# The residual of the first token half added by DMA in two down-projections

## The reference

```
x = x + m[2] * rmsnorm(mixer(h), g_post_mix)
h = modulate(rmsnorm(x, g_pre_ffn), m[3], m[4])
x = x + m[5] * rmsnorm(conv_ffn(h, w_up, w_dw, b_dw, w_down), g_post_ffn)

def conv_ffn(h, w_up, w_dw, b_dw, w_down):
    u = depthwise_conv(h @ w_up, w_dw) + b_dw
    gate, val = split(u, 2)
    return (silu(gate) * val) @ w_down       # 2816 -> 1024
```

## Time and profile before

| | |
|---|---|
| Median of 3 runs | 2520.65 us (2512.99 to 2523.09) |
| Profiled execution | 2511.87 us, span 2510.0 us |
| Mean granted PE clock | 0.990 |
| PE busy | 2420.9 us (96%), 11028 matmuls |
| DVE busy | 1955.5 us (78%) |
| ACT busy | 1259.4 us (50%) |
| POOL busy | 1036.8 us (41%) |
| DMA | 366.32 MB, mean 146 GB/s |

### The profile page before, as it was taken

One profiled execution on the slowest core, in us unless ns is written; L12 is line 12 of the kernel. 1 busy time (PEld: TensorE's weight loads), 2 busy tenths in 40 slices (PEclk: granted clock), 3 DMA queues, 4 the chain that ended last, 5 costly groups with the idle time before them and its releaser, 6 DMA issues.

```text
span 2510.0 us, 32042 instructions
## 1 busy us (share of the span) xinstructions
PE 2420.9 (96%) x11028; PEld 1937.1 (77%) x11028; DVE 1955.5 (78%) x2537; ACT 1259.4 (50%) x2062; POOL 1036.8 (41%) x731
## 2 busy tenths in 40 slices
PE   7989999999899999999999899999999999999997
PEld 3868888888687787888788687756877878887886
DVE  4467676667648999999655879997679999996556
ACT  3356665666544555555554442244645555555542
POOL 0057677882043566666200321000435666662002
PEclk9999999999999999999999999999999999999999
DMA  6046465651531354456975577611213544559755
GB/s 267 27 143 176 136 174 155 178 151 51 180 118 51 112 142 132 126 126 135 266 238 170 172 200 188 149 34 68 101 51 108 144 135 126 126 132 268 232 173 176
DMA packets 153204, 366.32 MB, mean 146 GB/s; under 512 B 14432, under 2 KB 15712, under 8 KB 153056
## 3 DMA queue, kind: packets, MB, share of 16 engines
q1 hardware_dynamic: 107056, 242.69, 27.5%
q0 software_dynamic: 44416, 116.93, 21.7%
q10 hardware_dynamic: 1584, 4.85, 0.6%
HBM read 303.07 MB, written 136.31 MB: 175 GB/s over the span
## 4 chain that ended last, share of the span: by engine, by line
PE 45%; DVE 38%; issue 7%; POOL 4%; ACT 3%; DMA 3%; SPq 0%; ACTq 0%; DVEq 0%; POOLq 0%
DVE weights_f32r L1998 13%; PE psum L2277 13%; PE psum L2279 12%; PE psum L2278 12%; DVE low L1975 3%; DVE acts L2187 3%; DVE acts L2189 3%; DVE low L1967 3%; DVE low L1965 2%; PE psum L2493 2%; ACT weights_f32r L976 1%; POOL set L837 1%; DMA set<-mod_w 1%; DVE weights_f32r L1862 1%; PE psum L2482 1%
## 5 line engine op out<-in xcount | busy, mean ns | idle before, releaser
L2277 PE MATMUL psum<-acts_f32r,weights_f32r 128*128 128x512 f32 x1536 | 610.0, 397 | 20.6 <-DVE low L2031 6.6
L2279 PE MATMUL psum<-acts_f32r,weights_f32r 128*128 128x512 f32 x1536 | 600.0, 391 | 0.0
L2278 PE MATMUL psum<-acts_f32r,weights_f32r 128*128 128x512 f32 x1536 | 599.7, 390 | 0.0
L976 ACT ACTIVATE weights_f32r<-low 128x512 fp32r<-128x512 f32 (+2 forms) x471 | 307.3, 659 | 336.0 <-PE psum L2279 159.2
L1998 DVE TENSOR_TENSOR weights_f32r<-low,weights_f32r 128x512 fp32r<-128x512 f32 x264 | 405.2, 1579 | 1.3
L862 POOL TENSOR_TENSOR low<-low 128x512 f32<-128x512 f32 x91 | 134.7, 1481 | 654.0 <-ACT low L1215 647.6
L2277 PEld LDWEIGHTS psum<-acts_f32r,weights_f32r 128*128 128x128 f32 x1536 | 289.4, 188 | 87.5 <-DVE weights_f32r L2004 7.7
L2279 PEld LDWEIGHTS psum<-acts_f32r,weights_f32r 128*128 128x128 f32 x1536 | 289.3, 188 | 61.5
L2278 PEld LDWEIGHTS psum<-acts_f32r,weights_f32r 128*128 128x128 f32 x1536 | 289.6, 189 | 60.6 <-issue 2.4
L889 POOL TENSOR_TENSOR low<-low 128x512 f32<-128x512 f32 x150 | 258.3, 1723 | 39.8 <-DVE acts_f32r L1983 29.3
L2277 PE MATMUL psum<-high_f32r,weights_f32r 128*128 128x512 f32 (+1 forms) x485 | 195.2, 403 | 16.2 <-ACT low L976 12.7
(11 more groups left out here) (254 smaller groups left out, 4944.4 us busy)
## 6 DMA issues: line engine op xcount, KB each, us to landing
low<-units SPq DMA_DIRECT2D x130, 512.0 KB, 4.9
set<-mod_w POOLq DMA_DIRECT2D x80, 512.0 KB, 3.9
low<-gated_sums SPq DMA_DIRECT2D x110, 256.0 KB, 4.5
low<-weight_sums SPq DMA_DIRECT2D x88, 256.0 KB, 4.2
gated_sums<-low SPq DMA_DIRECT2D x22, 768.0 KB, 3.5
low<-units SPq DMA_DIRECT2D x66, 256.0 KB, 5.0
weight_sums<-units POOLq DMA_DIRECT2D x14, 1024.0 KB, 10.3
residual<-low SPq DMA_DIRECT2D x48, 256.0 KB, 2.0
```

The lines of the kernel that those rows point to most:

```text
L976: return act.activation(out, in_, ACT.Copy, scale=scale)
L2277: pe.matmul(out, wl, xh, start=first, stop=False, skip_group_check=continued)
L2278: pe.matmul(out, wh, xl, start=False, stop=False, skip_group_check=continued)
L2279: return pe.matmul(out, wh, xh, start=False, stop=last, skip_group_check=continued)
```

## The change

In `down(b)` POOL now issues, for each block k of half 0, a DMA that adds the block of `xs_d` onto `A_half(k, 0)`, after three waits: the stores of the stream have landed, the block is renewed (`y_scaled`), and DMA k - 2 has landed. For b = 1 blocks 0 to 2 stand at the first x square of half 0 and block k + 2 ahead of POOL's addition of square k; for b = 3 all eight stand ahead of the additions of half 1. The semaphores `mod_in` become `pool_in` and count on. DVE's `add_residual(b, 0, k)` for b = 1 and 3 and SP's `load_residual(b, 0)` for them go. ACT's `x_square` and SP's `store_x` wait, by `residual_added`, for the DMA's landing where they waited for DVE. `X_BEFORE` gives the counts of DVE's remaining additions.

```
--- before.py
+++ after.py
@@ -263,6 +263,7 @@
 
 
 Y_BEFORE = (0, 16, 20, 36)
+X_BEFORE = {(0, 0): 0, (0, 1): 8, (1, 1): 16, (2, 0): 24, (2, 1): 32, (3, 1): 40}
 SQ_INDEX, SQ_FREED, SQ_SUMS, STAT_BEFORE = squares()
 T_BASE = {key: CB * n for n, key in enumerate([(0, 0), (0, 1), (1, 0), (1, 1), ("ln", 0), ("ln", 1), (2, 0), (2, 1)])}
 
@@ -335,7 +336,7 @@
         silu_c = sem("silu_c")
         scale_in = [sem(f"scale_in{j}") for j in range(CB // 2)]
         shift_in = [sem(f"shift_in{k}") for k in range(CB)]
-        mod_in = [sem(f"mod_in{s}") for s in range(2)]
+        pool_in = [sem(f"pool_in{s}") for s in range(2)]
         mod_acc, mod_mm, mod_out = sem("mod_acc"), sem("mod_mm"), sem("mod_out")
         ht_ready, h_act, h_hi, h_lo = sem("ht_ready"), sem("h_act"), sem("h_hi"), sem("h_lo")
         latent_in, mmx_done, lat_scaled, lat_hi, lat_lo = (
@@ -529,6 +530,13 @@
                 engine.wait_ge(s, value)
 
 
+        def residual_added(engine, b, half, k):
+
+            if (b, half) in X_BEFORE:
+                engine.wait_ge(x_new, X_BEFORE[b, half] + (k // 2 if b == 3 else k) + 1)
+            else:
+                engine.wait_ge(pool_in[k % 2], 16 * (5 * CB + b // 2 * CB // 2 + k // 2 + 1))
+
         KP = [(0, HALF), (HALF, HALF), (2 * HALF, CTX)]
 
 
@@ -638,7 +646,7 @@
                 if b == 3 and half and k % 2:
                     sp.wait_ge(x_pool, k // 2 + 1)
                 else:
-                    sp.wait_ge(x_new, 16 * b + CB * half + (k // 2 if b == 3 and half else k) + 1)
+                    residual_added(sp, b, half, k)
                 dst = outT if b == 3 else xs_d
                 sp.dma_start(dst[k][:, half * HALF:(half + 1) * HALF], A_half(k, half)).then_inc(x_out, 16)
 
@@ -724,10 +732,6 @@
                         store_g(layer, FB - 1)
                     if i == 9:
                         store_negated(layer, FB - 1)
-                    if t == 1 and j == 4:
-                        sp.wait_ge(mm_done, op_done(layer, MAIN - 1, 6))
-                        sp.wait_ge(x_out, 16 * 16 * b)
-                        load_residual(b, 0)
                     if t == 6 and 1 <= j < 9:
                         store_x(b, 0, j - 1)
                 if b == 1:
@@ -823,10 +827,10 @@
 
             for t in range(10):
                 for k in range(2):
-                    pool.dma_start(f(F_MD + k * L), modw[t + 2, k]).then_inc(mod_in[k], 16)
+                    pool.dma_start(f(F_MD + k * L), modw[t + 2, k]).then_inc(pool_in[k], 16)
                 acc = mod_acc_at(t)
                 for k in range(CB):
-                    pool.wait_ge(mod_in[k % 2], 16 * (1 + t * CB // 2 + k // 2))
+                    pool.wait_ge(pool_in[k % 2], 16 * (1 + t * CB // 2 + k // 2))
                     part = f(F_MD + (k % 2) * L)
                     if k == 0:
 
@@ -841,7 +845,7 @@
                             add.then_inc(mod_acc, 1)
                             pool.wait_ge(mod_acc, t + 1)
                     if k + 2 < CB:
-                        pool.dma_start(part, modw[t + 2, k + 2]).then_inc(mod_in[k % 2], 16)
+                        pool.dma_start(part, modw[t + 2, k + 2]).then_inc(pool_in[k % 2], 16)
                     if (t * CB + k) % 3 == 2 and t * CB + k < 72:
                         weight_sum(0, (t * CB + k) // 3)
 
@@ -952,7 +956,20 @@
 
             def down(b):
 
+                def add_residual(k):
+
+                    pool.wait_ge(x_out, 16 * 16 * b)
+                    pool.wait_ge(y_scaled, 16 * b + k + 1)
+                    if k > 1:
+                        residual_added(pool, b, 0, k - 2)
+                    pool.dma_start(A_half(k, 0), xs_d[k][:, 0:HALF], accum_op=ADD, max_dma_last_dim=4 * HALF).then_inc(pool_in[k % 2], 16)
+
                 for half, c, k in DOWN_ORDER[b]:
+                    if (half, c, k) == ((0, "x", 0) if b == 1 else (1, "y", 0)):
+                        for n in range(3 if b == 1 else CB):
+                            add_residual(n)
+                    if b == 1 and half == 0 and c == "x" and 0 < k < 6:
+                        add_residual(k + 2)
                     add_square(b, half, c, k)
 
             mixer(0)
@@ -965,7 +982,7 @@
             down(3)
             for k in range(1, CB, 2):
                 pool.wait_ge(y_scaled, 16 * 3 + CB + k + 1)
-                pool.wait_ge(blk_in[k], 16 * 9)
+                pool.wait_ge(blk_in[k], 16 * (2 + X_BEFORE[3, 1] // CB))
                 pool.tensor_tensor(A_half(k, 1), A_half(k, 1), x_res(3, 1, k), ADD).then_inc(x_pool, 1)
 
         @block.scalar
@@ -1234,7 +1251,7 @@
 
             def x_square(b, half, k):
 
-                act.wait_ge(x_new, 16 * b + CB * half + k + 1)
+                residual_added(act, b, half, k)
                 square(A_half(k, half), b, half, "x", k)
 
             def t_part(b, half, k, dst, shift):
@@ -1889,7 +1906,7 @@
             def add_residual(b, half, k):
 
                 dve.wait_ge(y_scaled, 16 * b + CB * half + k + 1)
-                dve.wait_ge(blk_in[k], 16 * (2 + 2 * b + half))
+                dve.wait_ge(blk_in[k], 16 * (2 + X_BEFORE[b, half] // CB))
                 dve.tensor_tensor(A_half(k, half), A_half(k, half), x_res(b, half, k), ADD).then_inc(x_new, 1)
 
             def renew_start(b, half):
@@ -2092,7 +2109,6 @@
                 def renewed(k):
 
                     renew(b, 0, k)
-                    add_residual(b, 0, k)
 
                 for i in range(6, ITEMS + 4):
                     t, j = divmod(i, KB)
```

More of the change, by code:

```diff
@@ L953, in down, with add_residual @@
             def down(b):
-                for half, c, k in DOWN_ORDER[b]:
+                def add_residual(k):
+                    pool.wait_ge(x_out, 16 * 16 * b)
+                    pool.wait_ge(y_scaled, 16 * b + k + 1)
+                    if k > 1:
+                        residual_added(pool, b, 0, k - 2)
+                    pool.dma_start(A_half(k, 0), xs_d[k][:, 0:HALF], accum_op=ADD, max_dma_last_dim=4 * HALF).then_inc(pool_in[k % 2], 16)
+                for half, c, k in DOWN_ORDER[b]:
+                    if (half, c, k) == ((0, "x", 0) if b == 1 else (1, "y", 0)):
+                        for n in range(3 if b == 1 else CB):
+                            add_residual(n)
+                    if b == 1 and half == 0 and c == "x" and 0 < k < 6:
+                        add_residual(k + 2)
                     add_square(b, half, c, k)
```

14 lines of the change are left out of this document (5 added, 9 removed).

## The result

The changed kernel takes 2526.68 us (median of 20 runs, 2519.21 to 2537.29), the kernel before 2517.15 us over its 20 runs (2507.20 to 2528.32). The ratio is 1.0037 with a 95% interval of 1.0025 to 1.0049, so it is slower by 0.37%, about 9.3 us. The profiled execution has a span of 2522.2 us against 2510.0, 12.2 us more. Lines have moved: L2048 is the combination of partial sums (L2031 before), L2021 and L2026 are the operand splits (L2004, L2009), L1903 the renewal (L1886), L965 the new DMA.

The account below looks back on a forecast made before the run. DVE was taken to bound the seam between sixth and seventh product, where PE waits for its combination. Terms 8.3 + 0.7 + 0 + 0.8 + 0.9 = +10.7 us, added to the median 2520.65, gave 2531.4 us, range 2516 to 2543.

Parts of the forecast that it names:

- The chain of landings: Layer 0: ACT's squares wait for three DMA landings in a row, so the combination L2031 starts 8.3 us later.
- port term: Layer 0: POOL's additions of squares slow DVE's splits by about 0.3 us each, two or three on the chain, +0.7 us.
- the prize: Both seams: removing DVE's 16 additions could save at most PE's waits and slow matmuls, 4.1 + 1.7 + 2.5 = 8.3 us.
- L: Time from issue to landing of POOL's adding DMA, taken as 5.5 us from L915's medians; bounds 4.0 and 7.4.
- Item 65: Layer 0, end of sixth product: PE waits some 2.6 us for this item, time it would wait at L2031 anyway.
- Everything behind ... shifts as it is: Behind layer 0's seam, renewed clock, spread and the convolution projection's input hang on PE's position and shift unchanged.
- Layer 1: SP's stores wait for the landing ahead of loads; PE's wait stays about what it is: 0, between -2.5 and +6 us.
- The clock: Layer 1: after a wait near 4 us PE's clock may fall too; half of 1.7, +0.9 us.
- The 0.8 us for the last group: Layer 1: the last group's loads, behind store 7, may cost +0.8 us.
- A short landing: Rival: same chain, landing at 2.0 us like a plain store's, so -6.4 us, 2514 us; chance 0.16.
- the break-even: Layer 0: the landing time at which the combination L2031 starts no later than before, 2.7 us.
- Landings of 7.4 us or more: Rival: DMA engines fill up and stores delay loads in both layers; +21 us, 2542 us; chance 0.16.

Follow-up runs that it names:

- both late: Changed kernel with SP's first-half stores (both layers) and ACT's x squares (layer 0) two items later; ratio 0.9994 to the kernel before.
- the control: Kernel before, DVE still adding, with SP's stores (both layers) and ACT's x squares (layer 0) two items later; ratio 1.0003 to the kernel before.
- two DMAs per block: Changed kernel with each 256 KB adding DMA issued as two of 128 KB, both landed before anything goes on; ratio 1.0044 to the kernel before.
- additions 4 to 6 deferred: Kernel before with DVE's additions and ACT's squares of blocks 4 to 6 behind the combination, stores two items later; 2510.29 us, ratio 0.9972.

## Why the prediction was right, point by point

**Right in kind and size, with some luck in the size:** +0.43% forecast, +0.37% measured, inside 0.5%. The chain of landings, the main term, came as forecast. The sum of +10.7 us fits because smaller terms were wrong both ways: a port term that did not come, and 3.6 us of slow matmuls in layer 0 that were not in it. The forecast time of 2531.4 us lies 4.7 us above the measured one, 3.5 of them because the three runs that it starts from had a higher median (2520.65) than the 20 (2517.15).

**What bounds the seam.** That DVE's additions held PE up, and that the prize was 8.3 us at most: 8.1 us without them.

**The chain in layer 0.** The form 3L plus a constant held. The constant from the rows of before was 1387.55 - 1376.08 = 11.47; measured 11.28. L was taken as 5.5; the three intervals have a mean of 5.4. This is closer than it deserves: L was defined, and read off L915, from the issue to the landing, but the sum starts it at the end of the renewal, and POOL issued 0.5 us after that. From issue to square the three took 3.79, 6.24 and 4.57 us, 4.9 in the mean. L was 0.6 us too long and the 0.5 us was left out. The combination was predicted 8.3 us later and came 7.8 later. L915 was a good proxy: landing 4.0, 5.0, 7.4 (least, median, most) there, 3.8, 5.4, 8.0 here. The estimate of 2.6 us by the fit of the Trainium skill, "DMA: Bandwidth & Descriptors", section on the anatomy of one DMA on the GpSimd path, does not hold for these accumulations: the shortest landing was 3.8 us.

**The port term, +0.7: wrong in this kernel.** No split ahead of the combination lasts longer than 0.69 us. Two of POOL's three additions of squares there fell into gaps in which DVE waited for ACT anyway, and the third ran beside a renewal that took its usual 0.74 us. They bite where DVE has no gaps (both late), and then harder than the 0.3 us that the prediction read off L1893. The kernel before already had a nearer row, a split beside POOL's 8.10 us of additions from 1397.80:

```profile
1401.26 1.78 DVE L2009 TENSOR_TENSOR set_f32r<-low,set_f32r 128x512 fp32r<-128x512 f32 x1
```

**Item 65:** a wait of 2.6 us was forecast and was 1.4, since the first interval was 4.3 and not 5.5 us; it only moved time from the other wait, as said.

**"Everything behind ... shifts as it is": wrong by 3.6 us in the profiled execution.** PE's timeline:

```profile
1402.95 0.79 PE L2293 MATMUL psum<-acts_f32r,weights_f32r 128*128 128x512 f32 x1 [10.18 <-DVE low L2048]
...
1408.66 0.51 PE L2294 MATMUL psum<-acts_f32r,weights_f32r 128*128 128x512 f32 x1
...
1441.32 0.50 PE L2293 MATMUL psum<-high_f32r,weights_f32r 128*128 128x512 f32 x1 [3.53 <-DVE weights_f32r L1879]
...
1446.17 1.59 PE L2594 MATMUL psum<-ones,low 128*128 128x1 f32 x8 [2.51 <-POOL low L866]
...
1448.19 0.63 PE L2294 MATMUL psum<-high_f32r,weights_f32r 128*128 128x512 f32 x1
...
2473.87 0.63 PE L2293 MATMUL psum<-acts_f32r,weights_f32r 128*128 128x512 f32 x1
```

From the first split to L2602's spread of the next statistics (1451.61 after, 1441.57 before) the way grew from 65.49 to 76.86 us, 11.4. Of this 7.8 is the later combination. At the start of the normalisation (L1935, 1426.91; before 1419.30) it was 8.9: PE ran at the lower rate for 5.7 us behind the wait of 10.2 us, where before it was 3.8 us behind 4.1, and that cost 1.2 us more. The last 2.4 us arise behind it. PE waits twice here, for L1879 and for POOL's sums. Before, its matmuls ran at the lower rate after the first wait, where the second wait swallowed that. After, they ran at the full rate there, PE waited 2.5 us instead of 1.2, and was slow behind it, where nothing covers it (0.63 us a matmul from 1448.19 on). The runs do not tell why the lower rate came at another place. The time from PE's sums to the spread was 3.0 us in the kernel before and in the control, 3.8 with two DMAs per block, 4.3 with additions 4 to 6 deferred and 5.4 to 5.7 in the other eight kernels, after waits of 0.7 to 2.5 us for POOL. Three of those eight have no DMA addition in layer 0. So this loss is not special to the change, and one profiled execution of each does not tell whether it goes with the kernel or with the execution.

**Layer 1.** The wait was forecast to stay between 2.5 and 4.5 us: 3.7. In the sum it stood with no change, and the way grew by 1.2 us. The mechanism, stores ahead of loads, is in the timelines of SP, ACT and DVE:

```profile
2459.31 0.34 SPq L651 DMA_DIRECT2D out_t<-low  x1
2459.70 0.42 SPq L683 DMA_DIRECT2D low<-weight_sums  x1
...
2461.68 0.34 SPq L651 DMA_DIRECT2D out_t<-low  x1
...
2464.63 0.63 ACT L993 ACTIVATE weights_f32r<-low 128x512 fp32r<-128x512 f32 x1 [7.02 <-DMA low<-weight_sums]
...
2470.41 0.63 ACT L993 ACTIVATE set_f32r<-low 128x512 fp32r<-128x512 f32 x1 [1.55 <-DMA low<-gated]
...
2472.34 2.47 DVE L2048 TENSOR_TENSOR low<-acts,psum 128x512 f32<-128x512 f32 x4
```

Store 0 waits 4.6 us for the landing, item 68's weights are issued behind it at 2459.70, and ACT waits 7.02 us for them. What was mis-sized is the landing of the loads: item 69's second load was issued at 2462.66 and ACT could copy it at 2470.41, 7.7 us later, where 3.9 was taken and 2 added for fuller engines. The clock did fall after 3.7 us (granted 0.50, 0.63 us a matmul from 2473.87 to 2477.28, 8 x 0.2 = 1.6 us), for which half a chance, 0.9, was in the sum. The 0.8 us for the last group did not appear: no wait of PE there.

**The sum** of the profiled execution: 11.4 in layer 0's seam and the next one (7.8, 1.2 and 2.4), 2.9 from layer 1's first split to the end (1.2 longer way, 1.6 clock), -1.3 ahead of layer 0's seam and -0.7 between the two, which no cause of the change explains: 12.3 us, against the 12.2 of the two spans.

**The rivals.** A short landing did not come: the least was 3.8 us, the break-even 2.7. Landings of 7.4 us or more came, up to 8.0, but not on the chain of layer 0. With the stores moved, one interval from renewal to square reached 7.7 us.

## What to carry to other kernels

An operation handed from a busy engine to a DMA costs nothing only if nobody in an in-order queue waits for its landing ahead of work that others need. Count the landings that stand one behind the other, multiply by the landing of the nearest DMA in the trace, add the time until its issue and the work that stands between them, and compare with the way before: here 3 x 5.4 (issue and landing) + 11.3 = 27.5 us against 19.7. Before moving work to another engine, try moving it behind the instruction that is waited for: three deferred additions gave nearly the whole prize with no DMA at all. Then look who waits for what was moved: a fourth, that of block 3, held POOL up and PE waited 3.3 us for it.

## What the runs showed of the hardware

An accumulation by DMA into on-chip memory takes about the same as one from memory to memory, 1.6 us of the 16 engines per 256 KB against 0.86 for plain transfers (51.6% of 28 us for 4.40 MB), and 0.87 us of issue on POOL. Its landing varied between 3.8 and 8.0 us after the issue in one kernel. More loads beside it went with a longer landing in one pair of rows (3.79 and 5.55 us), but the busy share of the engines did not order the others. A DVE split of 0.69 us lasted 1.78 us beside POOL's additions in the kernel before, and up to 2.5 us with both moves.

PE went on at its full rate (granted clock 1.00 in 2462.67 to 2466.00, the level of 2.4 GHz) after the wait of 2.5 us in layer 1 of the kernel before, and at about half of it (granted 0.50 to 0.51, the level of 1.2 GHz) for 3.4 to 5.7 us after waits of 3.7, 4.1 and 10.2 us. At the wait of 3.5 us for L1879 the two kernels differ: slow behind it before, at the full rate in the changed kernel, where it became slow only behind the next wait, of 2.5 us and some 5 us later. So the length of the last wait alone does not say at which rate PE goes on.
